# Two fused transformer blocks on one core: five places moved where one stage hands over to the next

## The chip, the cores and the metric

The kernel runs on one core of one Trainium2 chip. The metric is the device time of one execution in microseconds (us), as the median of several runs. All data is 32-bit.

## The reference, cut to what matters

Two blocks follow each other on 512 tokens of width 2048. Each block normalises its input, multiplies it with one very wide matrix, runs several mixers on slices of the product, and projects back.

```
# first block
p = rms_norm(x) @ w_in;  slices: lru, mlstm (u, o, z, ig, fg), moba (q, k, v, z)
ig = ig_pre + bi;  lf = log_sigmoid(fg_pre + bf)          # mlstm's two gates, 4 heads
uc = silu(causal_conv(u));  q, k = block_diag(uc, ..);  v = block_diag(u, ..)
x = x + concat(y_lru, y_ml, y_mo) @ w_out;  x = x + memory_cross_attention(x);  x = rms_norm(x)
# second block
proj = rms_norm(x) @ w_in_2;  slices: pool, swa, gla, mem, and g_logits (4 x 2048 columns)
y_c = gla_mixer(..)
gates = sigmoid(g_logits + b_merge)
merged = gates[0] * (y_a @ w_br_pool) + gates[1] * (y_b @ w_br_swa)
       + gates[2] * (y_c @ w_br_gla) + gates[3] * (y_m @ w_br_mem)
x = x + rms_norm(merged @ w_out_2)
```

## The kernel before, in words

**Split products.** Every large product is made in three passes. A weight tile `raw` (128 x 1024 numbers) is rounded by ScalarE (ACT) to `w_hi`; the rest, `w_lo = raw - w_hi`, is made by GpSimd (POOL, `low_rows`) in most stages and by VectorE (DVE, `w_low`) in the gate stage. The activations are split likewise into `ht_hi` and `ht_lo` (or `yh` and `yl`). TensorE (PE) then adds hi*hi, hi*lo and lo*hi.

**The ring.** `raw`, `w_hi` and `w_lo` have four slots each (`RING`). The tiles are numbered through the whole program (`PHASES`, `H4`), tile j lies in slot j % 4. `hi_done` counts ACT's roundings, `lo_done` the rests, `half_done` the tiles that PE has finished. SyncE (SP) issues the loads of `raw`, each when the rest of the tile four before it is made. Each engine has its own queue in program order, written by hand; no scheduler changes it. `PHASES` also counts, for each stage, the results that go through the two banks `proj0` and `proj1` in turn; `bank_free` counts when ACT or DVE has emptied them.

**The stages around the change**, in order of time:

- *mlstm, first pair of heads.* PE makes unit 0 and unit 1 of the projection; behind tile 9 of unit 1, `gate_picks` writes the two gates' rows to banks S0 and S1. ACT adds their bias (`r_ig`, `r_f`), takes the absolute value, the exponential and the logarithm (`r_b`, event `ln`), and only then the tanh of the convolved tile (`ml_th(0)`, line 1807) whose chunk DVE turns into `m_uc` (event `uc0`, line 2858). PE waits for `ln` and for `uc0` before `ml_qkv(0)` (line 928), which writes S0, S1 and S2.
- *zg, the branch product of the gla mixer.* Sixteen units of 8 tiles of contraction. The first three are begun on 6 tiles each (`early`: `proj0`, `proj1`, `t1`), since the last head's output is not there yet. `gla_out(3)`, eight transposes of `g_o`, stands behind the first of them. Behind the transposes DVE and ACT make the last two tiles of `yh` and `yl`. Unit 15 lies in `proj0`, the same bank into which the next stage, swa, puts its first unit; ACT empties each unit to `z_early` (line 2261) and spills it.
- *zp, the branch product of the pool mixer,* sixteen units, emptied to `z_late` (the fourth of each to `dist`, line 2261).
- *The gate stage.* g_logits is made in 32 pairs of column blocks. A pair takes seven products of half size (p1, p5, p6, p3, p7, p2, p4, line 1536) in place of eight, on sums of weight blocks (`t_w`) that DVE makes. ACT rounds the blocks and sums (`right_high`, `left_high`, lines 2493, 2497, 2527), DVE makes their rests (line 3559). Pairs use two sets of banks in turn. ACT rounds the three first tiles of pair 0 after it has emptied unit 15 of zp.
- *The closing product* merged @ w_out_2 (line 1582), 32 tiles in four blocks `fb` of 8 tiles `kp`. Its left operand `ht_hi`, `ht_lo` is `merged`, rounded by ACT (`merged_highs`, line 2567) and DVE (`lows`, line 3050). SP issues its first four loads after all of `gate_loads`, thus after the last `z_tile`. ACT rounds the first four tiles in the last pair (`merged_half`, line 2562), POOL makes their rests, and from tile 4 on ACT goes on after `phase_end`, at which ACT and DVE wait for each other.

The events of pair t that matter here: `lb11`, `lb22`, `lt3`, `lb21` say that slots 0, 1, 2 and 3 of `raw` have been read for the last time (for an odd b, slots 1 and 2 in this order).

Of the kernel before, what the change touches and what calls it, by code (L numbers as in the profile page):

```python
# [12 lines left out]
P = 128  # L13
T = 512
# [34 lines left out]
          ("xq", 8, 4), ("xwo", 8, 16), ("gv", 16, 2), ("gla", 32, 16), ("zg", 16, 16), ("swa", 80, 40),  # L49
# [80 lines left out]
def build(nc, a, out, stop=None):  # L130

    with ExitStack() as ctx:
# [376 lines left out]
        def _(sp):  # L509
# [151 lines left out]

            def gate_loads(m, b, first, last):
# [3 lines left out]
                if not last:  # L666
                    wait(sp, st_dve, "lb11", t)
                    gate_block(nm, nb, 0, 0, 0, block_in[0])
                    wait(sp, st_dve, "lb22", t + 1)
                    gate_block(nm, nb, slots[0], 0, 1, block_in[slots[0]])  # L670
                    wait(sp, st_dve, "lt3", t + 1)
                    gate_block(nm, nb, slots[1], 1024, 1, block_in[slots[1]])
# [6 lines left out]
                if not last:  # L679
                    wait(sp, st_dve, "lb21", t + 1)  # L680
                    gate_block(nm, nb, 3, 1024, 0, block_in[3])
# [11 lines left out]
            for fb in range(4):  # L693
                for kp in range(8):
                    j = 8 * fb + kp
                    if j < RING:
                        wait(sp, st_dve, ("lb11", "lb22", "lt3", "lb21")[j], PAIRS - 1 if j == 0 else PAIRS)
                    sp.wait_ge(lo_done, th(H4["wout2"], j) - RING)
                    sp.dma_start(raw[:, j % RING, :].rearrange("p (k n) -> p k n", n=T),
                                 a["w_out_2"][0][256 * kp:256 * kp + 256, T * fb:T * fb + T].rearrange(  # L700
                                     "(k p) n -> p k n", p=P)).then_inc(raw_ready[j % RING], 16)
# [7 lines left out]
        def _(pool):  # L709
# [34 lines left out]
            with pool.Fori(1, NH // RING) as i:  # L744
                low_rows(i)
# [3 lines left out]
        def _(pe):  # L749
# [155 lines left out]
            for pr in range(ML_PAIRS):  # L905
# [98 lines left out]
                if pr == 0:  # L1004
                    wait(pe, mlg_act, "ln")
# [355 lines left out]
            for u, bank in enumerate(early):  # L1361
# [4 lines left out]
                if u == 0:  # L1366
                    gla_out(GLA_HEADS - 1)
# [4 lines left out]
            with pe.Fori(1, 4) as i:  # L1372
                for u in range(4):
                    branch_unit(i + b, u, i * 2 + qb, u - 1, yh, yl)

# [230 lines left out]
        def _(act):  # L1606
# [174 lines left out]
            for pr in range(ML_PAIRS):  # L1781
# [90 lines left out]
                ml_th(0)  # L1872

                ml_ahead(2)
                ml_qv(0)
                ml_u(1)

                ml_th(1)
# [1828 lines left out]
```

## Time and profile before

| | |
|---|---|
| median of 3 runs | 3238.24 us (3236.93 to 3241.14) |
| the profiled execution's own time | 3237.58 us |
| its span, first to last instruction | 3235.8 us |
| PE busy | 3207.2 us, 99% |
| DVE, ACT, POOL busy | 1263.3, 1262.4, 1077.5 us |
| TensorE's granted clock, mean | 0.998 |
| share of PE in the chain that ended last | 96% |

PE is the engine that all others feed. "Busy" of PE is the time in which at least one matmul is in flight, so what the change could alter is PE's idle time, 28.6 us in all, and the rate of its matmuls. The list of waits names each of PE's pauses with the instruction that ended it; the chain that ended last gives start and length of each piece of work; the windows view gives the granted clock of a stretch, where 1.00 is 2.4 GHz and 0.50 is 1.2 GHz.

### The profile page before, as it was taken

The page shows a single profiled execution, that of the slowest core. Times are in us where ns is not written, and L with a number is a line of the kernel's source. Part 1 is how long each engine was busy: PE and PEld are TensorE (multiplying, and loading weights), DVE is VectorE, ACT ScalarE, POOL GpSimd, SP SyncE. Part 2 cuts the span into 40 slices and gives each one's busy share as a digit, 9 for nine tenths or more (in the row PEclk, how much of TensorE's full clock was granted, in tenths as well). Part 3 has the DMA queues.
Part 4 walks back from the last instruction along what each step waited for, and adds up shares of the span by engine and source line. Part 5 has one row for each costly group of instructions (what it writes and reads, how often), then busy time and mean ns, then how long its engine had stood idle before and what let it go on. Part 6 is the DMA issues. An engine that isn't in the chain of part 4 may idle for free.

```text
span 3235.8 us, 45156 instructions
## 1 busy us (share of the span) xinstructions
PE 3207.2 (99%) x17218; PEld 2757.1 (85%) x17218; DVE 1263.3 (39%) x1717; ACT 1262.4 (39%) x1928; POOL 1077.5 (33%) x464
## 2 busy tenths in 40 slices
PE   9999999999999999999999999999999999999999
PEld 8877888888888888888888888888889999999887
DVE  3573321112124544302110111135448888878701
ACT  6543322333236544332332333322334444444432
POOL 6633333434442434344343343444520000000143
PEclk9999999999999999999999999999999999999999
DMA  7622322323442423243332232423544444444442
GB/s 284 181 78 66 85 70 81 86 83 99 122 121 82 138 77 89 84 140 88 85 98 84 83 98 79 150 84 91 172 127 131 131 130 130 130 130 133 135 155 98
DMA packets 546541, 364.52 MB, mean 113 GB/s; under 512 B 18808, under 2 KB 505208, under 8 KB 545144
## 3 DMA queue, kind: packets, MB, share of 16 engines
q1 hardware_dynamic: 522912, 321.50, 34.1%
q10 hardware_dynamic: 23512, 41.40, 3.7%
q8 instruction: 81, 1.33, 0.2%
q14 instruction: 36, 0.29, 0.0%
HBM read 333.49 MB, written 29.36 MB: 112 GB/s over the span
## 4 chain that ended last, share of the span: by engine, by line
PE 96%; DVE 1%; ACT 1%; DMA 1%; issue 1%; POOL 0%; DVEq 0%; ACTq 0%; SPq 0%; POOLq 0%
PE proj L765 59%; PE s L1536 10%; PE t L1536 8%; PE s L1582 3%; PE s L1237 1%; PE proj L1582 1%; PE t L1582 1%; PE proj L1536 1%; PE t L790 1%; PE s L834 1%; PE s L827 1%; PE t L1237 1%; PE proj L1237 1%; PE s L1062 1%; PE s L1043 1%
## 5 line engine op out<-in xcount | busy, mean ns | idle before, releaser
L739 POOL TENSOR_TENSOR w_lo<-raw,w_hi 128x1024 fp32r<-128x1024 f32 x435 | 1075.4, 2486 | 2132.4 <-ACT w_hi L1619 1440.3
L765 PE MATMUL proj<-ht_hi,w_hi 128*128 128x512 f32 x2400 | 955.5, 398 | 0.7 <-ACT z_early L2261 0.7
L765 PE MATMUL proj<-ht_hi,w_lo 128*128 128x512 f32 x2400 | 935.5, 390 | 0.0
L765 PE MATMUL proj<-ht_lo,w_hi 128*128 128x512 f32 x2400 | 934.5, 389 | 0.0
L1619 ACT ACTIVATE w_hi<-raw 128x1024 fp32r<-128x1024 f32 x396 | 404.3, 1053 | 386.8 <-PE proj L765 223.3
L765 PEld LDWEIGHTS proj<-ht_hi,w_hi 128*128 128x128 f32 x2400 | 450.8, 188 | 95.8 <-issue 4.8
L765 PEld LDWEIGHTS proj<-ht_hi,w_lo 128*128 128x128 f32 x2400 | 450.4, 188 | 95.7
L765 PEld LDWEIGHTS proj<-ht_lo,w_hi 128*128 128x128 f32 x2400 | 451.0, 188 | 94.9 <-issue 4.6
L3559 DVE TENSOR_TENSOR w_lo<-raw,w_hi 128x1024 fp32r<-128x1024 f32 x128 | 156.4, 1222 | 73.0 <-ACT w_hi L2527 43.3
L1536 PE MATMUL s<-ht_hi,w_hi 128*128 128x256 f32 x512 | 145.4, 284 | 3.6 <-DVE w_lo L3559 3.6
L1536 PE MATMUL s<-ht_hi,w_lo 128*128 128x256 f32 x512 | 145.5, 284 | 0.0
L2497 ACT ACTIVATE w_hi<-t_w 128x1024 fp32r<-128x1024 f32 x96 | 101.4, 1057 | 112.7 <-DVE t_w L3575 58.4
L1536 PE MATMUL s<-ht_lo,w_hi 128*128 128x256 f32 x512 | 145.3, 284 | 0.0
L3559 DVE TENSOR_TENSOR w_lo<-t_w,w_hi 128x1024 fp32r<-128x1024 f32 x96 | 117.5, 1224 | 69.5 <-ACT w_hi L2497 69.5
L2493 ACT ACTIVATE w_hi<-raw 128x1024 fp32r<-128x1024 f32 x96 | 101.6, 1058 | 77.0 <-PE s L1536 38.9
L1536 PE MATMUL t<-ht_hi,w_lo 128*128 128x256 f32 x384 | 108.6, 283 | 0.0
L1536 PE MATMUL t<-ht_hi,w_hi 128*128 128x256 f32 x384 | 108.6, 283 | 0.0
L1536 PE MATMUL t<-ht_lo,w_hi 128*128 128x256 f32 x384 | 108.5, 282 | 0.0
L1536 PE MATMUL s<-s_hi,w_hi 128*128 128x256 f32 x384 | 108.1, 281 | 0.0
L1536 PE MATMUL s<-s_lo,w_hi 128*128 128x256 f32 x384 | 108.0, 281 | 0.0
L1536 PE MATMUL t<-s_hi,w_hi 128*128 128x256 f32 x384 | 108.0, 281 | 0.0
L1536 PE MATMUL t<-s_lo,w_hi 128*128 128x256 f32 x384 | 107.9, 281 | 0.0
(654 smaller groups left out, 5431.8 us busy)
## 6 DMA issues: line engine op xcount, KB each, us to landing
raw<-in_w_in_dram SPq DMA_DIRECT2D x404, 512.0 KB, 3.6
raw<-in_w_out_dram SPq DMA_DIRECT2D x64, 512.0 KB, 3.9
g_zt<-z_spill SPq DMA_DIRECT2D x64, 256.0 KB, 2.8
raw<-in_xa_wkv_dram SPq DMA_DIRECT2D x16, 512.0 KB, 7.7
raw<-in_w_mem_kv_dram SPq DMA_DIRECT2D x16, 512.0 KB, 3.8
raw<-in_w_br_gla_dram SPq DMA_DIRECT2D x16, 512.0 KB, 4.0
z_spill<-z_early ACTq DMA_DIRECT2D x32, 256.0 KB, 3.1
raw<-in_w_br_pool_dram SPq DMA_DIRECT2D x16, 512.0 KB, 4.2
```

What stands on the lines that cost most here:

```text
L739: pool.tensor_tensor(w_lo[:, slot, :], raw[:, slot, :], w_hi[:, slot, :].bitcast(F32), ALU.subtract).then_inc(lo_done, 1)
L765: ins = pe.matmul(dst, w, x[:, kt, c0:c1], start=first and n == 0 and m == 0, stop=last and n == len(kts) - 1 and m == 2)
L790: ins = pe.transpose(dst[0:m, n * P:n * P + k], src, ident[0:k, 0:k])
L827: pe.matmul(MEM_V[x][blk][:], h[:, kt, c0 + blk * P:c0 + blk * P + P], w, start=kt == 0 and m == 0, stop=kt == KT - 1 and m == 2)
L834: ins = pe.matmul(MEM_K[x][hd // 2][:, hd % 2 * M:hd % 2 * M + M], w, h[:, kt, c0:c0 + M], start=kt == 0 and hd % 2 == 0 and m == 0, stop= ...
L1237: ins = pe.matmul(VB[blk][t][:], x[:, kt, t * P:(t + 1) * P], w, start=kt == 0 and m == 0, stop=kt == KT - 1 and m == 2)
L1536: ins = pe.matmul(dst, w, x[:, k, :], start=fresh and k == 0 and m == 0, stop=k == 7 and m == 2, skip_group_check=True)
L1582: ins = pe.matmul(BANKS[fb % 2][t][:], x[:, k, t * P:(t + 1) * P], w, start=k == 0 and m == 0, stop=k == KT - 1 and m == 2)
L1619: act.activation(w_hi[:, slot, :], raw[:, slot, :], ACT.Copy).then_inc(hi_done, 1)
L2493: return act.activation(w_hi[:, (PRODUCTS * b + j) % RING, :], src, ACT.Copy)
L2497: return act.activation(w_hi[:, (PRODUCTS * b + j) % RING, :], t_w[:], ACT.Copy)
L3559: return dve.tensor_tensor(w_lo[:, slot, :], src, w_hi[:, slot, :].bitcast(F32), SUB)
```

## The change

1. **First gate pair.** ACT rounds the three first tiles of pair 0 behind units 12, 13 and 14 of zp, one each, in place of behind unit 15.
2. **Closing loads.** In the last pair, SP issues the first four loads of `w_out_2` one by one, each at the event that frees its slot, among the `z_tile` loads. The rests of these four tiles are made by DVE, not by POOL, which waits until they are made.
3. **Tanh ahead.** ACT makes `ml_th(0)` and rounds two tiles before the exponential and the logarithm; PE no longer waits for `ln`.
4. **Transposes.** `gla_out(3)` stands behind the second early unit.
5. **Bank.** Unit 15 of zg goes to `t1`; the two-bank stages count two units fewer, and the loop of zg is one turn shorter, its last turn written out.

```diff
-("zg", 16, 16)
+("zg", 16, 14)
@@ SP @@
-                if not last:
-                    wait(sp, st_dve, "lb11", t)
-                    gate_block(nm, nb, 0, 0, 0, block_in[0])
...
+                def load(slot, k0, n):
+                    if last:
+                        out_rows(slot)
+                    else:
+                        gate_block(nm, nb, slot, k0, n, block_in[slot])
+                wait(sp, st_dve, "lb11", t)
+                load(0, 0, 0)
+                wait(sp, st_dve, "lb22", t + 1)
+                load(slots[0], 0, 1)
+                wait(sp, st_dve, "lt3", t + 1)
+                load(slots[1], 1024, 1)
...
                 z_tile(m, b, 1)
+                wait(sp, st_dve, "lb21", t + 1)
+                load(3, 1024, 0)
...
-            for fb in range(4):
-                for kp in range(8):
...
+            for j in range(RING, 32):
+                sp.wait_ge(lo_done, th(H4["wout2"], j) - RING)
+                out_rows(j)
@@ POOL @@
-            with pool.Fori(1, NH // RING) as i:
+            with pool.Fori(1, H4["wout2"]) as i:
+                low_rows(i)
+            pool.wait_ge(lo_done, th(H4["wout2"], 3))
+            with pool.Fori(H4["wout2"] + 1, NH // RING) as i:
                 low_rows(i)
@@ PE @@
-                if pr == 0:
-                    wait(pe, mlg_act, "ln")
                 ml_qkv(0)
...
-                if u == 0:
+                if u == 1:
                     gla_out(GLA_HEADS - 1)
...
-            with pe.Fori(1, 4) as i:
+            with pe.Fori(1, 3) as i:
                 for u in range(4):
                     branch_unit(i + b, u, i * 2 + qb, u - 1, yh, yl)
+            for u in range(3):
+                branch_unit(b + 3, u, qb + 6, u - 1, yh, yl)
+            pe.wait_ge(z_apart, 1)
+            accumulate(b + 3, 3, TB[1][:], range(8), 0, yh, yl, (0, T), True, True)
@@ ACT @@
                     link(act.activation(r_b[0:4, :], r_f[0:4, :], ACT.Abs))
+                ml_th(0)
+
+                ml_ahead(2)
+                if pr == 0:
                     link(act.activation(r_b[0:4, :], r_b[0:4, :], ACT.Exp, scale=-1.0))
                     act.activation(r_b[0:4, :], r_b[0:4, :], ACT.Ln, bias=ones[0:4, 0:1]).then_inc(mlg_act.sem, 1)
-                ml_th(0)
-
-                ml_ahead(2)
...
+                    elif shift and isinstance(i, int) and i == 3 and u == 3:
+                        z_kept(st, TB[1], z_apart, 2, u, i * 4 + branch * KT + u, i + used)
...
-            act.sem_inc(bank_free[1], 1)
...
                     branch_z("zp", BR_POOL, i, (u,), 12, z_late)
+                    if 4 * i + u == 12:
+                        right_high(0, 0, B11, EARLIER + 16, block_in[0]).then_inc(st_act.sem, 9)
+                    elif 4 * i + u in (13, 14):
+                        wait(act, st_dve, ("t1", "t2")[u - 1], 0)
+                        left_high(0, u).then_inc(st_act.sem, u)
...
-            for slot in range(3):
-                act.wait_ge(half_done, th(H4["zp"], 12 + slot))
...
@@ DVE @@
-            lows(xy, HT_MERGED, 0.5, range(4))
+            def out_low(j):
+                dve.wait_ge(hi_done, th(H4["wout2"], j))
+                dve.tensor_tensor(w_lo[:, j, :], raw[:, j, :], w_hi[:, j, :].bitcast(F32), SUB).then_inc(lo_done, 1)
+            out_low(0)
+            out_low(1)
+            lows(xy, HT_MERGED, 0.5, range(2))
+            out_low(2)
+            lows(xy, HT_MERGED, 0.5, range(2, 4))
             corner(3, PAIRS, 4)
+            out_low(3)
             gated(1, GROUPS - 1, 3, PAIRS, 4, 1)
```

**ACT's queue at the end of zp and the start of the gate stage, before.** `z_late` and `dist` rows empty units 13, 14 and 15, each `DMA` spills one; L2493 and L2497 are `right_high` and `left_high`. The brackets name the semaphores that a row waits for (`x_in0` is the landing of the first weight block, `st_dve` is DVE's count of the gate stage).

```order
L2261 ACTIVATE z_late<-proj 128x512 [waits mem0_in1,half_done]
L2263 DMA z_spill<-z_late 128x512 [waits bank_free1]
L2261 ACTIVATE z_late<-proj 128x512 [waits mem0_in2,half_done]
L2263 DMA z_spill<-z_late 128x512 [waits bank_free0]
L2261 ACTIVATE dist<-proj 128x512 [waits mem0_in3,half_done]
L2263 DMA z_spill<-dist 128x512 [waits bank_free1]
L2493 ACTIVATE w_hi<-raw 128x1024 [waits x_in0,half_done]
L2497 ACTIVATE w_hi<-t_w 128x1024 [waits st_dve,half_done] x2
L2493 ACTIVATE w_hi<-raw 128x1024 [waits x_in2,half_done]
```

The same place of the changed program (line numbers of its own):

```order
L2276 DMA z_spill<-z_late 128x512 [waits bank_free0]
L2501 ACTIVATE w_hi<-raw 128x1024 [waits x_in0]
L2274 ACTIVATE z_late<-proj 128x512 [waits mem0_in1,half_done]
L2276 DMA z_spill<-z_late 128x512 [waits bank_free1]
L2505 ACTIVATE w_hi<-t_w 128x1024 [waits st_dve]
L2274 ACTIVATE z_late<-proj 128x512 [waits mem0_in2,half_done]
L2276 DMA z_spill<-z_late 128x512 [waits bank_free0]
L2505 ACTIVATE w_hi<-t_w 128x1024 [waits st_dve]
L2274 ACTIVATE dist<-proj 128x512 [waits mem0_in3,half_done]
L2276 DMA z_spill<-dist 128x512 [waits bank_free1]
L2501 ACTIVATE w_hi<-raw 128x1024 [waits x_in2,half_done]
```

The first three roundings have moved ahead of the emptying of units 13, 14 and 15; the fourth stays behind it.

**ACT's queue at the gates of mlstm, before.** `ACT_TABLE_LOAD` is the switch between function tables that the compiler puts in.

```order
L1869 ACTIVATE r_b<-r_f 4x512 [waits act_chain]
L1870 ACT_TABLE_LOAD
L1870 ACTIVATE r_b<-r_b 4x512 [waits act_chain]
L1871 ACT_TABLE_LOAD
L1871 ACTIVATE r_b<-r_b,ones 4x512 [waits act_chain]
L1807 ACT_TABLE_LOAD
L1807 ACTIVATE m_h<-m_uc 128x512 [waits ml_conv]
L1619 ACTIVATE w_hi<-raw 128x1024 [waits half_done,raw_ready2]
L1619 ACTIVATE w_hi<-raw 128x1024 [waits half_done,raw_ready3]
L1815 ACTIVATE m_q<-s 128x512 [waits ml_pe]
L1803 ACTIVATE m_up<-proj 128x512 [waits ml_dve,ml_pe,half_done]
L1807 ACTIVATE m_h<-m_uc 128x512 [waits ml_conv]
```

And of the changed program:

```order
L1881 ACTIVATE r_b<-r_f 4x512 [waits act_chain]
L1819 ACT_TABLE_LOAD [waits ml_conv]
L1819 ACTIVATE m_h<-m_uc 128x512 [waits act_chain]
L1631 ACTIVATE w_hi<-raw 128x1024 [waits half_done,raw_ready2]
L1631 ACTIVATE w_hi<-raw 128x1024 [waits half_done,raw_ready3]
L1886 ACTIVATE r_b<-r_b 4x512
L1887 ACT_TABLE_LOAD
L1887 ACTIVATE r_b<-r_b,ones 4x512 [waits act_chain]
L1827 ACTIVATE m_q<-s 128x512 [waits ml_pe]
L1815 ACTIVATE m_up<-proj 128x512 [waits ml_dve,ml_pe,half_done]
L1819 ACT_TABLE_LOAD
L1819 ACTIVATE m_h<-m_uc 128x512 [waits ml_conv]
```

Three table switches stay three, but only one now stands ahead of the first tanh, and it carries the wait for the convolution (`ml_conv`) itself. The exponential has none of its own any more.

**DVE's queue at the end of the last gate pair, before.** L3624 and L3626 are the last two sums of the pair, L3050 the rests of `merged`, L3583 the corner sum that needs p4.

```order
L3624 TENSOR_TENSOR t<-t,dist 128x256 [waits st_act,st_pe]
L3626 TENSOR_TENSOR t<-t,dist 128x256 [waits st_pe]
L3050 SCALAR_TENSOR_TENSOR ht_lo<-xy,ht_hi 128x512 [waits norm_hi] x4
L3583 TENSOR_TENSOR t<-proj,sn_188 128x256 [waits st_pe]
L3593 SCALAR_TENSOR_TENSOR g_zt_187<-gate_e,g_zt_187 128x512 [waits z_in1,st_act]
L3595 TENSOR_TENSOR xy<-xy,g_zt_187 128x512 [waits st_dve]
```

And of the changed program:

```order
L3635 TENSOR_TENSOR t<-t,dist 128x256 [waits st_act,st_pe]
L3637 TENSOR_TENSOR t<-t,dist 128x256 [waits st_pe]
L3653 TENSOR_TENSOR w_lo<-raw,w_hi 128x1024 [waits hi_done] x2
L3061 SCALAR_TENSOR_TENSOR ht_lo<-xy,ht_hi 128x512 [waits norm_hi] x2
L3653 TENSOR_TENSOR w_lo<-raw,w_hi 128x1024 [waits hi_done]
L3061 SCALAR_TENSOR_TENSOR ht_lo<-xy,ht_hi 128x512 [waits norm_hi] x2
L3594 TENSOR_TENSOR t<-proj,sn_188 128x256 [waits st_pe]
L3653 TENSOR_TENSOR w_lo<-raw,w_hi 128x1024 [waits hi_done]
L3604 SCALAR_TENSOR_TENSOR g_zt_187<-gate_e,g_zt_187 128x512 [waits z_in1,st_act]
```

Four rests of weight tiles, POOL's before, stand in DVE's queue among the rests of `merged` and around the corner sum.

## Rows read from the trace of the kernel before

**Rows 1.** The page: POOL's rests and the commonest matmul; busy us, mean ns of one, idle before.
```profile
L739 POOL TENSOR_TENSOR w_lo<-raw,w_hi 128x1024 fp32r<-128x1024 f32 x435 | 1075.4, 2486 | 2132.4 <-ACT w_hi L1619 1440.3
L765 PE MATMUL proj<-ht_hi,w_hi 128*128 128x512 f32 x2400 | 955.5, 398 | 0.7 <-ACT z_early L2261 0.7
```
**Rows 2.** The list of PE's waits: line, what ended it, us in total, times, longest.
```profile
PE s L1582 <- DVE ht_lo L3050: 4.8, 1, 4.8
PE s L928 <- DVE m_uc L2858: 4.1, 1, 4.1
PE s L1536 <- DVE w_lo L3559: 3.6, 1, 3.6
...
PE s L790 <- DVE g_o L3244: 1.7, 1, 1.7
...
PE proj L765 <- ACT z_early L2261: 0.7, 1, 0.7
```
**Rows 3.** Windows of 2 us: PE, PEld, DVE, ACT, POOL busy, granted clock, DMA share, GB/s.
```profile
248.00:250.00 2.00, 2.00 (x4) 0.91 (x3) 0.00 (x0) 0.00 (x0) 2.00 (x2) 0.50 0.00 0
1372.00:1374.00 2.00, 1.23 (x10) 1.19 (x11) 0.81 (x3) 0.00 (x0) 0.00 (x0) 1.00 0.00 0
2408.00:2410.00 2.00, 2.00 (x11) 2.00 (x11) 0.80 (x2) 1.22 (x2) 0.00 (x0) 0.50 0.67 200
3054.00:3056.00 2.00, 2.00 (x6) 1.53 (x5) 2.00 (x1) 1.85 (x3) 1.72 (x2) 0.50 0.33 126
```
**Rows 4.** The chain that ended last (start, us): first and second gate pair's opening part.
```profile
2406.35 21.72 PE s L1536 x168
...
2448.07 20.00 PE s L1536 x168
```
**Rows 5.** Timeline of DVE and ACT at the end of zp (start, us).
```profile
2377.63 2.85 DVE L3565 TENSOR_TENSOR t_w<-raw 128x1024 f32<-128x1024 f32 x1 [15.42 <-DMA raw<-in_w_in_dram]
...
2403.89 1.06 ACT L2493 ACTIVATE w_hi<-raw 128x1024 fp32r<-128x1024 f32 x1 [0.49 <-ACT dist L2261]
```
**Rows 6.** The chain that ended last, closing product: its first load, blocks fb 0 and 2.
```profile
3041.60 6.49 DMA raw<-in_w_out_dram
...
3052.86 45.38 PE s L1582 x192
...
3141.75 43.52 PE s L1582 x192
```
**Rows 7.** Timeline of DVE and ACT in and behind the last gate pair.
```profile
3029.80 1.22 DVE L3559 TENSOR_TENSOR w_lo<-raw,w_hi 128x1024 fp32r<-128x1024 f32 x1
...
3049.70 2.18 ACT L2567 ACTIVATE ht_hi<-xy 128x512 fp32r<-128x512 f32 x4
...
3063.39 4.90 DVE L3050 SCALAR_TENSOR_TENSOR ht_lo<-xy,ht_hi 128x512 fp32r<-128x512 f32 x8
```
**Rows 8.** Timeline of ACT and DVE at the gates of mlstm, and a switch in lru.
```profile
210.67 1.28 ACT L1746 ACT_TABLE_LOAD   x1 [2.37 <-PE proj L765]
...
239.46 2.33 DVE L2751 SCALAR_TENSOR_TENSOR m_uc<-m_up,par,m_uc 128x512 f32<-128x512 f32 x3
...
243.75 1.28 ACT L1807 ACT_TABLE_LOAD   x1
245.04 0.63 ACT L1807 ACTIVATE m_h<-m_uc 128x512 f32<-128x512 f32 x1
245.71 0.69 DVE L2858 SCALAR_TENSOR_TENSOR m_uc<-m_h,m_uc 128x512 f32<-128x512 f32 x1 [3.92 <-ACT m_h L1807]
```
**Rows 9.** The chain that ended last: `ml_qkv(0)` of the first and of the second pair.
```profile
246.54 4.51 PE s L928 x6
...
374.93 2.58 PE s L928 x6
```
**Rows 10.** Timeline of DVE behind the transposes of `gla_out(3)`.
```profile
1373.90 1.41 DVE L3253 SCALAR_TENSOR_TENSOR y_f<-s,par,g_z 128x512 f32<-128x512 f32 x2 [1.19 <-PE s L790]
1375.36 1.35 DVE L3258 TENSOR_TENSOR yl<-y_f,yh 128x512 fp32r<-128x512 f32 x2
```

More of the change, by code:

```diff
@@ L48 @@
 PHASES = [("kv", 32, 2), ("lru", 16, 8), ("ml", 36, 18), ("moba", 48, 24), ("wout", 32, 16),
-          ("xq", 8, 4), ("xwo", 8, 16), ("gv", 16, 2), ("gla", 32, 16), ("zg", 16, 16), ("swa", 80, 40),
+          ("xq", 8, 4), ("xwo", 8, 16), ("gv", 16, 2), ("gla", 32, 16), ("zg", 16, 14), ("swa", 80, 40),
           ("mem", 16, 8), ("zs", 8, 16), ("pool", 32, 16), ("zm", 8, 16), ("zp", 16, 16), ("wout2", 32, 16)]
@@ L660, in _, with out_rows @@
                 gate_block(0, 0, slot, k0, n, block_in[slot])
+            def out_rows(j):
+                fb, kp = j // 8, j % 8
+                sp.dma_start(raw[:, j % RING, :].rearrange("p (k n) -> p k n", n=T),
+                             a["w_out_2"][0][256 * kp:256 * kp + 256, T * fb:T * fb + T].rearrange(
+                                 "(k p) n -> p k n", p=P)).then_inc(raw_ready[j % RING], 16)
             def gate_loads(m, b, first, last):
@@ L665, in gate_loads @@
                 slots = (2, 1) if b % 2 == 0 else (1, 2)
-                if not last:
-                    wait(sp, st_dve, "lb11", t)
-                    gate_block(nm, nb, 0, 0, 0, block_in[0])
[L669 to L672, printed above, removed]
+                def load(slot, k0, n):
[9 more added lines that the diff above has]
+                load(slots[1], 1024, 1)
                 if first:
@@ L678, in gate_loads @@
                 z_tile(m, b, 1)
-                if not last:
-                    wait(sp, st_dve, "lb21", t + 1)
-                    gate_block(nm, nb, 3, 1024, 0, block_in[3])
+                wait(sp, st_dve, "lb21", t + 1)
+                load(3, 1024, 0)
                 if not first:
@@ L692, in _ @@
                 gate_loads(GROUPS - 1, b, False, b == 3)
-            for fb in range(4):
-                for kp in range(8):
[L695 to L701, printed above, removed]
+            for j in range(RING, 32):
+                sp.wait_ge(lo_done, th(H4["wout2"], j) - RING)
+                out_rows(j)
             for n, (t, c0, c1) in enumerate(OUT_PARTS):
@@ L2482, in sums_high @@
                 act.activation(sums[n][0], sums[n][1], ACT.Copy).then_inc(sums_hi, 1)
-            for i in range(4):
-                for u in range(4):
-                    branch_z("zp", BR_POOL, i, (u,), 12, z_late)
-                    if 3 <= 4 * i + u < 7:
-                        sums_high(4 * i + u - 3)
             def right_high(b, j, src, value, landed):
@@ L2502, in gate_tanh @@
                                       bias=par[:, bass.ds(m * 2 + x + PARAM["b_merge"] + b * KT, 1)])
-            for slot in range(3):
-                act.wait_ge(half_done, th(H4["zp"], 12 + slot))
-                if slot == 0:
-                    right_high(0, 0, B11, EARLIER + 16, block_in[0]).then_inc(st_act.sem, 9)
-                else:
-                    wait(act, st_dve, ("t1", "t2")[slot - 1], 0)
-                    left_high(0, slot).then_inc(st_act.sem, slot)
+            for i in range(4):
+                for u in range(4):
+                    branch_z("zp", BR_POOL, i, (u,), 12, z_late)
+                    if 3 <= 4 * i + u < 7:
+                        sums_high(4 * i + u - 3)
+                    if 4 * i + u == 12:
[3 more added lines that the diff above has]
+                        left_high(0, u).then_inc(st_act.sem, u)
             def gate_pair(m, b, first=False, last=False):
```

## The prediction

> **What bounds the kernel now.** PE has work in flight for 3207.2 of 3235.8 us, so nothing can be won on the other engines except where PE waits for them. I read four views in this order. First the page, for the shape of a matmul [rows 1]. Then the list of PE's waits: five pauses lie at the places that the change touches, 4.8, 4.1, 3.6, 1.7 and 0.7 us, 14.9 us together, half of PE's 28.6 us of idle time [rows 2]. Then the granted clock behind each pause, which the wait list does not show: it is 0.50 for some us behind the 4.1, 3.6 and 4.8 us pauses, so PE runs at 1.2 in place of 2.4 GHz there, but 1.00 behind the 1.7 us pause [rows 3]. Last the chain and the timelines at each place, for what a pause costs in the work behind it and for what would be late next.
>
> A second thing that the wait list hides: a matmul is 0.398 us long in the records [rows 1], but 192 of them take 43.52 us, 0.227 each [rows 6]. A pause is counted from the end of the last one, so closing it also takes back the overlap, 0.398 - 0.227 = 0.17 us. I use it for each pause that closes whole.
>
> **Part 1, first gate pair.** Today ACT empties unit 15, rounds the first tile at 2403.89 for 1.06 us, DVE makes the rest, and PE stands still for 3.6 us [rows 2, 5]. In the changed queue this rounding stands behind unit 12. A unit is 24 matmuls, some 5.5 us, so it starts three units earlier, near 2387. What it needs is there: DVE had both first weight blocks at 2377.63 and made their difference by 2380.5 [rows 5]. The two sums follow at units 13 and 14, again with 5.5 us for about 1.1 us of ACT and 2.4 of DVE, which has nothing else to do. So the pause goes, 3.6 + 0.17. Behind it the seven products of pair 0 took 21.72 us, those of pair 2 took 20.00 [rows 4]: 1.72 us of half clock, which goes too, since PE no longer stops. Together **5.5 us**. SP's loads of the next blocks move ahead with `lb11`, so nothing behind gets later.
>
> **Part 2, closing loads.** Now the first load of `w_out_2` is issued after the last `z_tile`, at 3041.6, and ACT cannot go on until the second has landed near 3048.1 [rows 6]. It then makes `ht_hi` at 3049.70 [rows 7], DVE the rest, PE waits 4.8 us [rows 2]. With the change the slot of tile 0 is free before the last pair begins (3028), and the slot of tile 1 at about 3031.0, when DVE has made the `lb22` rest that starts at 3029.80 [rows 7]; even at 6.5 us a load both are in by 3037.5. ACT may round tile 0 after p3 and tile 1 after p7, which ends two products of 20.00 / 7 us [rows 4] before p4, near 3042.4; DVE then makes its last sum of the pair. p4 ends at 3048.1 (3052.86 less 4.8) [rows 2, 6]. From there: tile 1 rounded by 3043.5, tanh 0.7, four `ht_hi` of 0.54 each [rows 7] by 3046.4. DVE is free from 3042.8: two rests of 1.22 us [rows 7] to 3045.2, then the first two `ht_lo` at some 0.6 us each, done by 3046.5. So there is 1.5 us to spare and the pause closes, 4.8 + 0.17. The first block of the closing product took 45.38 us against 43.52 of a later one [rows 6]: 1.86 us of half clock, gone as well. Together **6.8 us**. What is late next: the second `kp` needs `ht_lo` 2 and 3, which now stand behind the rest of tile 2. This tile can be rounded after p2 and the first four `ht_hi`, by 3047.4, so `ht_lo` 3 is done near 3049.8, and PE wants it 24 matmuls after 3048.1, at 3053.5. POOL's four rests leave a queue that did nothing else.
>
> **Part 3, tanh ahead.** The pause ends at 246.54 and was 4.1 us, so it began at 242.45 [rows 2, 9]. ACT went through two more table switches, exponential and logarithm before it could switch to tanh at 243.75 (1.28 us) and compute it (0.63 us); DVE's `m_uc` took 0.69 us, PE started 0.14 us later [rows 8]. The convolution that tanh needs was ready at 239.46 + 2.33 = 241.79 [rows 8]. In the new queue the one switch left carries the wait for it. A switch behind such a wait does not run ahead: in lru it began when PE was done [rows 8]. So 241.8 + 1.28 + 0.63 + 0.69 and 0.2 of hand-overs gives 244.6: the pause shrinks from 4.1 to 2.2 us, **1.9 us** won. Behind it `ml_qkv(0)` took 4.51 us at half clock against 2.58 at full [rows 3, 9], 1.93 us. Whether that is won depends on a pause of 2.2 us, which this trace does not have: 1.7 us did not lower the clock, 3.6 us did [rows 2, 3]. Between 0 and **1.9 us** I take 1.9, since 2.2 is nearer to 1.7. The exponential and logarithm end near 248.5 and are wanted only after the second convolution; if the clock stays up, ACT's copy of q comes 1.2 us after PE's products, beside unit 2's 10.9 us.
>
> On the price of a switch the Trainium skill differs (ScalarE: Activation LUTs, What ACT_TABLE_LOAD costs): it adds 1.38 us of drain to each switch, 2.66 us in all. By that figure the pause would stay at 3.5 us. The rows have no room for it: the load of 1.28 us at 243.75 is followed by tanh at 245.04 [rows 8]. The measurement decides.
>
> **Parts 4 and 5.** DVE's `g_o` came 1.7 us after PE's first early unit [rows 2]; now 18 matmuls of 0.227, 4.1 us, lie between, so the pause goes, 1.9 us with the overlap. Late next could be the last two `yl`: they were ready 2.8 us after the transposes (1373.90 to 1376.71) [rows 10], and one early unit of 4.1 us is left to cover them. It covers, with 1.3 us over. Unit 15 in `t1` frees `proj0` two units early, which ends the 0.7 us pause, 0.9 with the overlap. Together **2.8 us**. ACT, DVE and SP have the same rows as before there.
>
> **The sum.** 5.5 + 6.8 + 1.9 + 1.9 + 2.8 = 18.9 us off the profiled execution, 3237.6 to 3218.7. That execution lies 0.7 us under the median, so the forecast for the median is 3238.2 - 18.9 = **3219.3 us**.
>
> **The rivals.**
> *The clock falls behind the shortened mlstm pause.* For it: three of the four pauses I priced are followed by half clock, and 2.2 us is over the longest that was not. Against: it is much nearer to 1.7 than to 3.6. It costs 1.9 us: 3221.2. *A switch behind a wait costs a second length of itself,* some drain of the engine. Then the pause stays at 3.5 us and the clock falls as it did: 1.3 + 1.9 us over the forecast, 3222.5. The rows speak against it: the tanh starts 0.01 us after its switch [rows 8]. The drain that the Trainium skill gives (ScalarE: Activation LUTs, What ACT_TABLE_LOAD costs) would be this case.
> *One joint keeps its pause,* because a wait takes the removed one's place: the likeliest is the closing one, where three engines must all be on time with 1.5 us to spare. If its pause and clock stay whole, 3219.3 + 6.8 = 3226.1; if it is the gate pair, 3224.8. Each us of a partial failure costs one us.
> *It gets slower.* The place is tile 4 of the closing product. ACT rounds it only after `phase_end`, thus after DVE's whole queue, to which four rests are added (4.9 us). PE wants it 96 matmuls after 3048.1, at 3069.9; DVE's queue used to end at 3068.3 [rows 7], which with ACT's rounding of 1.06 and POOL's rest of 2.49 us [rows 1, 5] would come too late. But it used to start its rests of `merged` at 3050.4 and now starts at 3042.8, so I have its end at 3062. From about 3065.5 on each us is lost. It would take an end near 3090 to make the kernel slower than 3244.7, which needs DVE or a load to hang for 28 us. I see nothing that would.
> *The switch still runs ahead of its wait,* against what the queue says: then the pause is 0.9 us and the time 3218.0.
>
> **How the numbers follow.** All joints close and the clock stays up: 0.50, 3219.3. The clock falls after the mlstm pause: 0.28, 3221.2. The longer switch: 0.03, 3222.5. One joint keeps all or part of its pause: 0.12, 3222 to 3226.1. Switch ahead: 0.03. Slower: 0.02. Two hundredths are left for something unseen that eats most of the gain. The three runs of before spread over 4 us, so a median may sit 1.5 us off on either side. The range from 3216.0 to 3225.5 holds all cases but the rare ones and the whole failure of the largest joint. The measurement can tell 0.2%, 6.5 us, from no change. Every case but the last two lies below 3231.8: faster 0.94, same 0.04, slower 0.02.
>
> **What would show it.** In the list of PE's waits the entries for L1582, L1536, `g_o` and `z_early` are gone, and the one for `ml_qkv` reads 2.2 us. The first gate pair's opening part takes 20.0 us, the first closing block 43.5, `ml_qkv(0)` 2.6. PE's idle time falls from 28.6 to about 15.9 us. I am wrong if a new wait over 0.5 us stands at the third early unit of zg, at the second or fifth `kp` of the closing product, or if the granted clock still reads 0.50 behind a joint.

## The result, and the profile after

The changed kernel takes **3217.24 us** (median of 4 runs, 3216.34 to 3218.66), the kernel before beside it 3238.41 us (4 runs, 3236.93 to 3241.14): a ratio of 0.9934, 95% interval 0.9917 to 0.9951. The forecast was 3219.3 us with a range from 3216.0 to 3225.5. The profiled execution of the changed kernel took 3218.66 us with a span of 3216.5, that of before 3237.58 and 3235.8. So the traces differ by 19.3 us where the sum said 18.9. One later run of the kernel before, in the third set of experiments, was slow (3985.86 us at a mean granted clock of 0.752) and is left out of every median and ratio here.

The list of PE's waits after the change, in the columns of [rows 2]:

```profile
PE s L859 <- POOL small L739: 3.0, 1, 3.0
PE s L938 <- DVE m_uc L2869: 2.1, 1, 2.1
PE s L800 <- DVE ht_lo L2674: 0.9, 1, 0.9
PE t L800 <- ACT a_pt L1955: 0.5, 1, 0.5
PE s L800 <- DVE ht_lo L2682: 0.5, 1, 0.5
```

Of the five pauses of [rows 2], four are gone; `ml_qkv`'s is left with 2.1 us in place of 4.1. The 3.0 us at the top stood in the kernel before too, and so did, with 1.5 us, the third line: the chain leads there from the landing of one of the first weight tiles (`raw<-in_xa_wkv_dram`, at 38.17 us here and 38.98 before) through ACT and DVE to PE, and no part of the change is near. Below, this wait is called the first landing.

The chain that ended last (start us, us, what) says where each microsecond was won:

```profile
243.76 2.84 PE s L938 x6
246.60 10.90 PE proj L775 x48
...
370.48 2.58 PE s L938 x6
...
2395.40 19.99 PE s L1548 x168
...
2435.39 20.00 PE s L1548 x168
...
3035.39 43.55 PE s L1594 x192
...
3122.46 43.52 PE s L1594 x192
```

Such rows are read by how far each landmark lies ahead of the same one in before. The `ml_qkv(0)` of the second pair is 4.45 us earlier (374.93 to 370.48 [rows 9]); 0.81 us of it was there before mlstm began, from the first landing, so mlstm gave 3.64. The first gate pair begins 10.95 us earlier (2406.35 to 2395.40 [rows 4]). 2.91 us of that came in zg, and the rest, 3.6, is the gate pair's pause. The second gate pair is 12.68 us earlier (2448.07 to 2435.39), so the opening part behind the joint gave 1.73 more. The closing product starts 17.47 us earlier (3052.86 to 3035.39 [rows 6]), 4.79 from its own pause, and its block 2 is 19.29 us earlier (3141.75 to 3122.46), another 1.82 from the first block. PE's record of busy time fell from 3207.2 to 3201.1 us although it does the same matmuls. Most of these 6.1 us is work that ran at half clock, the rest mainly the overlap at each joint; no list of waits shows either.

ACT at the gates of mlstm in the changed kernel (start us, us, and in brackets the idle time ahead and what ended it), to be put beside [rows 8]:

```profile
238.31 0.63 ACT L1881 ACTIVATE r_b<-r_f 4x512 f32<-4x512 f32 x1
241.06 1.28 ACT L1819 ACT_TABLE_LOAD   x1 [2.11 <-DVE m_uc L2762]
242.35 0.63 ACT L1819 ACTIVATE m_h<-m_uc 128x512 f32<-128x512 f32 x1
242.88 1.99 ACT L1631 ACTIVATE w_hi<-raw 128x1024 fp32r<-128x1024 f32 x2
244.78 0.61 ACT L1886 ACTIVATE r_b<-r_b 4x512 f32<-4x512 f32 x1
245.41 1.28 ACT L1887 ACT_TABLE_LOAD   x1
```

ACT is idle for 2.11 us and only then loads its table: the load stands behind the wait for the convolution, as in lru. The exponential at 244.78, behind the tanh, has no load of its own; before the change it had one. The logarithm, with its load at 245.41, lies beside PE's products.

DVE and ACT in the last gate pair, same columns, beside [rows 7]:

```profile
3030.01 2.35 DVE L3653 TENSOR_TENSOR w_lo<-raw,w_hi 128x1024 fp32r<-128x1024 f32 x2
3032.28 1.28 DVE L3061 SCALAR_TENSOR_TENSOR ht_lo<-xy,ht_hi 128x512 fp32r<-128x512 f32 x2
...
3043.60 4.90 DVE L3061 SCALAR_TENSOR_TENSOR ht_lo<-xy,ht_hi 128x512 fp32r<-128x512 f32 x8
```
```profile
3031.20 2.18 ACT L2578 ACTIVATE ht_hi<-xy 128x512 fp32r<-128x512 f32 x4
3033.28 1.05 ACT L2573 ACTIVATE w_hi<-raw 128x1024 fp32r<-128x1024 f32 x1
```

The first two `ht_lo` are done at 3033.56, and in the chain PE's closing product starts at 3035.39, 1.8 us later (its first matmul is at 3035.23, 1.7 us later; the section on the prediction says where the difference comes from). DVE's queue ends at 3048.50.

### The profile page after: what moved, and what is told of

The parts are those of the page before. It is cut to its first block, busy times and chain, and to the rows that moved or that the text cites. A ratio compares the mean times of both kernels' runs of the same rounds, so it can differ in the third digit from the quotient of the medians.

```text
span 3216.5 us, 45137 instructions
## 1 busy us (share of the span) xinstructions
PE 3201.1 (100%) x17218; PEld 2754.0 (86%) x17218; DVE 1261.3 (39%) x1721; ACT 1262.4 (39%) x1928; POOL 1068.2 (33%) x460
## 4 chain that ended last, share of the span: by engine, by line
PE 97%; DVE 1%; DMA 1%; ACT 1%; issue 0%; POOL 0%; SPq 0%; DVEq 0%; ACTq 0%; POOLq 0%
PE proj L775 59%; PE s L1548 10%; PE t L1548 9%; PE s L1594 3%; PE proj L1548 1%; PE proj L1594 1%; PE s L1245 1%; PE t L1594 1%; PE t L800 1%; PE s L844 1%; PE s L837 1%; PE t L1245 1%; PE proj L1245 1%; DMA raw<-in_xa_wkv_dram 1%; PE s L1070 1%; PE s L1051 1%
```

## The experiments

Each set ran on one chip with the kernel before beside it: 3237.21 us in the first set, 3237.87 in the second, 3236.93 in the third. Medians of 5 or 6 runs; "pause" is the wait at the joint concerned, in the profiled execution.

| kernel | median us (range) | ratio to before (95%) | pause us |
|---|---|---|---|
| again | 3219.55 (3216.94 to 3220.70) | 0.9947 (0.9934 to 0.9961) | mlstm 2.1 |
| u_gate | 3224.16 (3222.21 to 3225.53) | 0.9961 (0.9948 to 0.9975) | gate pair 3.6 |
| u_close | 3227.19 (3224.60 to 3227.57) | 0.9969 (0.9957 to 0.9981) | closing 4.7 |
| u_tanh | 3222.13 (3221.20 to 3224.71) | 0.9955 (0.9942 to 0.9969) | mlstm 4.1 |
| u_zg | 3222.19 (3221.37 to 3223.28) | 0.9953 (0.9939 to 0.9966) | zg 1.7 and 0.7 |
| c_pool | 3218.74 (3217.77 to 3220.08) | 0.9941 (0.9928 to 0.9955) | closing none |
| p_two | 3221.39 (3220.95 to 3223.15) | 0.9950 (0.9937 to 0.9964) | mlstm 3.4 |
| x_sel | 3217.66 (3216.11 to 3217.94) | 0.9937 (0.9924 to 0.9951) | mlstm 1.7 |
| again2 | 3219.97 (3218.98 to 3220.15) | 0.9945 (0.9931 to 0.9959) | mlstm 2.1 |
| x_exp | 3217.30 (3215.62 to 3217.89) | 0.9936 (0.9922 to 0.9950) | mlstm 0.9 |
| x_both | 3217.11 (3215.61 to 3218.50) | 0.9938 (0.9924 to 0.9953) | mlstm 0.7 |

None of them leaves out any part of the reference. The sets are: again, u_gate, u_close and u_tanh on one chip; u_zg, c_pool, p_two and x_sel on a second; again2, x_exp and x_both on a third. The second set has no run of the changed kernel.

### again: the changed kernel once more, for the size of the scatter

> The changed kernel once more, beside the runs that undo one part each. Theory: each joint gives its pause, 0.17 us of overlap and, for pauses of 3.6 us and more, 1.7 to 1.9 us of half clock; ratio to before 0.994 (19 to 21 us). Rival: the fast runs of before and after differ by chance and the pauses alone count; then 14 us, ratio 0.9957.

3219.55 us, 2.3 over its median of the first measurement; its single runs go from 3216.94 to 3220.70. The gain over the kernel before is 17.7 us, under the 19 to 21 that were expected, and the interval of the ratio holds both the theory's 0.994 and the rival's 0.9957. So the medians do not decide between them. A difference of 1 us between two medians says nothing here, and the parts below are read from the traces first.

### u_gate: part 1 undone

```diff
-                    if 4 * i + u == 12:
-                        right_high(0, 0, B11, EARLIER + 16, block_in[0]).then_inc(st_act.sem, 9)
...
+            for slot in range(3):
+                act.wait_ge(half_done, th(H4["zp"], 12 + slot))
```

> Part 1 undone: the first three tiles of gate pair 0 are rounded behind unit 15 of zp again. Theory: 5.5 us over the changed kernel, a pause of 3.6 us and the first pair's opening part at 21.7 us with a granted clock of 0.50 in it. Rival, pauses alone count: 3.8 us over, opening part at 20.0. Rival, a later wait takes it up: under 2 us.

4.6 us over the changed kernel of the same set, and the pause of 3.6 us is back whole. The half clock behind it is not. The chain of u_gate:

```profile
243.08 4.22 PE s L938 x6
247.30 11.24 PE proj L775 x48
...
2399.99 20.24 PE s L1548 x168
```

Its windows of 2 us (as in [rows 3]), at mlstm and behind the gate pause:

```profile
244.00:246.00 2.00, 2.00 (x4) 0.86 (x3) 0.00 (x0) 1.98 (x3) 2.00 (x2) 0.60 0.00 0
...
2400.00:2402.00 2.00, 2.00 (x17) 2.00 (x18) 1.90 (x2) 0.00 (x0) 0.00 (x0) 1.00 0.44 97
2402.00:2404.00 2.00, 2.00 (x19) 2.00 (x18) 0.79 (x2) 1.57 (x2) 0.00 (x0) 1.00 0.57 166
```

Behind the same pause of 3.6 us, which in the profile of before had the clock down [rows 3, 4], the clock reads 1.00 here. The opening part is 0.25 us longer than the changed kernel's 19.99, and that is no half clock either: 0.16 of it is the overlap that the chain cuts off a piece that follows without a pause (see the section on the prediction), and the first matmul behind the pause is 0.36 us long in place of 0.28. The 2.1 us pause in mlstm, behind which the clock held in the changed kernel, cost 1.7 here: 4.22 against 2.84 in `ml_qkv(0)` and 11.24 against 10.90 in the piece behind it. So this execution fits the rival "pauses alone count" (3.8 us, opening part near 20.0) and not the theory's 5.5; the rest of what the profile is over comes from mlstm and from the first landing. What stands behind a pause of one length differs from profile to profile.

### u_close: part 2 undone

```diff
+                if not last:
+                    wait(sp, st_dve, "lb11", t)
+                    gate_block(nm, nb, 0, 0, 0, block_in[0])
...
-            out_low(0)
-            out_low(1)
-            lows(xy, HT_MERGED, 0.5, range(2))
...
+            lows(xy, HT_MERGED, 0.5, range(4))
```

> Part 2 undone whole: the four closing loads are issued behind the last z_tile, and POOL makes their rests. Theory: 6.8 us over the changed kernel, a pause of 4.8 us, first closing block 45.4 us. Rival, pauses alone count: 5.0 us over, first block 43.5 us.

7.6 us over the changed kernel of the set. Its wait at the closing product, and its chain:

```profile
PE s L1588 <- DVE ht_lo L3055: 4.7, 1, 4.7
```
```profile
3028.64 5.59 DMA raw<-in_w_out_dram
3039.79 45.45 PE s L1588 x192
3128.76 43.52 PE s L1588 x192
```

Read as in the prediction, 4.7 + 0.17 + 1.93 is 6.8, the size that it gave the part. Read by landmarks it is 6.6: u_close is 0.29 us ahead of the changed kernel inside the last gate pair (3015.10 against 3015.39) and 6.30 behind it at block 2 (3128.76 against 3122.46). The section on the prediction says where the 0.2 us between the two readings come from. The 1 us to 7.6 is within what medians scatter.

### u_tanh: part 3 undone

```diff
+                if pr == 0:
+                    wait(pe, mlg_act, "ln")
...
-                ml_th(0)
-
-                ml_ahead(2)
```

> Part 3 undone: exponential and logarithm ahead of the first tanh, and PE waits for the logarithm. Theory: 3.8 us over the changed kernel, pause 4.1 us in place of 2.1, ml_qkv(0) 4.5 us in place of 2.8 at a granted clock of 0.50. Rival, the clock is indifferent: 2.0 us over, ml_qkv(0) unchanged.

2.6 us over the changed kernel. The trace shows the pause of 4.1 us again, `ml_qkv(0)` at 4.51 us, and a granted clock of 0.60 and 0.55 in the two windows behind it: 2.0 us of pause and 1.7 of half clock, 3.7 in all. The median shows less. It may be that some executions of the changed kernel pay the half clock too, as u_gate above and c_pool below do at this place; but its own three profiles do not show it, so this is not shown.

### u_zg: parts 4 and 5 undone

```diff
-                if u == 1:
+                if u == 0:
...
-            pe.wait_ge(z_apart, 1)
-            accumulate(b + 3, 3, TB[1][:], range(8), 0, yh, yl, (0, T), True, True)
```

> Parts 4 and 5 undone: the transposes behind the first early unit, unit 15 of zg in proj0. Theory: 2.8 us over the changed kernel, pauses of 1.7 and 0.7 us back, granted clock 1.00 throughout there. Rival, the eight transposes only change places and the wait for the last two tiles of yl takes the pause over: 1 us over.

3222.19 us, 3.5 over c_pool of the same set, which has the changed kernel's joints. The 1.7 us before `g_o` and the 0.7 us before `z_early` are back. Against the trace of the changed kernel the two cost 2.9 us, so the rival of 1 us fell.

### c_pool: the closing loads early, but POOL makes the four rests

```diff
-            with pool.Fori(1, H4["wout2"]) as i:
-                low_rows(i)
-            pool.wait_ge(lo_done, th(H4["wout2"], 3))
-            with pool.Fori(H4["wout2"] + 1, NH // RING) as i:
+            with pool.Fori(1, NH // RING) as i:
...
-            out_low(0)
-            out_low(1)
```

> Half of part 2: the closing loads stay early, but POOL makes the rests of the first four tiles as before. Theory: the loads were what was late. POOL needs 2.5 us a rest, tile 0 is there by 3025, tile 1 some 0.3 us before p4 ends, so PE starts on time or at most 0.5 us late: 0 to 0.5 us over the changed kernel. Rival: the gain needs DVE, since POOL's passes and DVE's rests of merged slow each other (1.46 us each in place of 0.6 in the trace of before): pause of 1 to 3 us.

3218.74 us, no closing pause, first block 43.55 us. POOL's first rest ended at 3032.11 and not by 3025, early enough all the same, and the rival's pause of 1 to 3 us did not come. Part 2's gain is that of the loads. Moving the four rests to DVE is not needed for it, though it leaves more room: the first two `ht_lo` were done 0.9 us ahead of PE's first closing matmul, in place of 1.7. Beside POOL's rests DVE's first four `ht_lo` took 5.93 us here (timeline of DVE, then of POOL, in c_pool):

```profile
3033.61 5.93 DVE L3058 SCALAR_TENSOR_TENSOR ht_lo<-xy,ht_hi 128x512 fp32r<-128x512 f32 x4 [1.75 <-ACT ht_hi L2575]
3042.98 2.49 DVE L3058 SCALAR_TENSOR_TENSOR ht_lo<-xy,ht_hi 128x512 fp32r<-128x512 f32 x4
```
```profile
3032.55 2.41 POOL L746 TENSOR_TENSOR w_lo<-raw,w_hi 128x1024 fp32r<-128x1024 f32 x1 [0.45 <-ACT w_hi L2570]
3036.16 2.83 POOL L746 TENSOR_TENSOR w_lo<-raw,w_hi 128x1024 fp32r<-128x1024 f32 x1 [1.20 <-ACT w_hi L2570]
```

The next four, with POOL idle, took 2.49 us. Of the first four only two are long, 1.90 and 2.90 us; each ends some 0.55 us after one of POOL's rests. The two between them, which started with POOL idle, took 0.68 each. c_pool's windows behind its mlstm pause of 2.1 us show the clock down again:

```profile
244.00:246.00 2.00, 2.00 (x3) 0.67 (x2) 0.00 (x0) 1.98 (x3) 2.00 (x1) 0.50 0.00 0
246.00:248.00 2.00, 2.00 (x5) 0.87 (x3) 0.00 (x0) 1.28 (x2) 2.00 (x2) 0.65 0.24 40
```

In the changed kernel the same windows read 1.00:

```profile
244.00:246.00 2.00, 2.00 (x5) 0.81 (x5) 0.00 (x0) 1.98 (x3) 2.00 (x1) 1.00 0.00 0
246.00:248.00 2.00, 2.00 (x9) 1.50 (x8) 1.29 (x2) 1.99 (x4) 2.00 (x2) 1.00 0.17 36
```

Up to this place the two programs do the same work in the same order. Nor is it the chip: u_zg ran on the chip of c_pool, and again and u_close on that of u_gate, and in these three the clock held. The six products of `ml_qkv(0)` took 4.54 us in c_pool and 2.84 in the changed kernel.

### p_two: the tanh of the first pair made three times

```diff
-                ml_th(0)
+                ml_th(0, 2 if pr == 0 else 0)
```

> A doubled cost: the tanh of ml_th(0) is made three times over in the first pair, which lengthens PE's pause there from 2.1 to 3.4 us and changes nothing else. Theory, the length of the pause decides the clock: at 3.4 us the granted clock falls to 0.50 behind it as it did at 3.6, and the kernel is 1.3 + 1.9 = 3.2 us over the changed one. Rival, the clock falls behind the heavy engine switch only at 3.6 us and more: 1.3 us over, ml_qkv(0) still 2.8 us.

The pause is 3.4 us, 1.3 longer, which is two tanh of 0.63, so ACT's work there is on the path one to one; `ml_qkv(0)` took 4.54 us and the clock read 0.92, 0.50 and 0.73 in the three windows from 244 to 250. The median, 3221.39, is 2.65 us over that of c_pool. The run does not say that the length of the pause decides: behind 2.1 us, in c_pool, the clock fell as well and `ml_qkv(0)` took the same 4.54 us.

### x_sel: two small preparations of DVE behind the first convolution

```diff
-            link.inc(dve.tensor_copy(i_r[:], ident[:]))
-            link.inc(dve.tensor_tensor(r_sel[:], ident[:, 0:4], ident[:, 32:36], ADD))
...
+                if pr == 0:
+                    link.inc(dve.tensor_copy(i_r[:], ident[:]))
+                    link(dve.tensor_tensor(r_sel[:], ident[:, 0:4], ident[:, 32:36], ADD))
```

> A further step: DVE's two small tiles (i_r, r_sel, 2.5 us, of which r_sel 2.35 beside POOL) go behind the first convolution. Theory: PE's pause before ml_qkv(0) is bound by the convolution's end at 241.0; it starts 2.4 us earlier, then ACT's absolute value at 238.9 and the switch are last, and the pause falls from 2.1 to under 0.2 us: 2.0 us under the changed kernel. Rival: POOL's passes slow the convolution too where it now runs beside them (2.33 us for three passes becomes 4 or more), and the pause stays at 1 us or over.

A miss: the pause went from 2.1 only to 1.7 us. `r_sel` is an addition of 128x4 numbers that takes 2.35 us where it stands, so to take it off the path should have been worth 2. But once it is moved, the next instruction is as long. DVE in x_sel:

```profile
234.05 2.68 DVE L2760 TENSOR_SCALAR m_uc<-m_up,par 128x512 f32<-128x512 f32 x1
236.77 2.33 DVE L2762 SCALAR_TENSOR_TENSOR m_uc<-m_up,par,m_uc 128x512 f32<-128x512 f32 x3
...
241.87 0.16 DVE L2942 TENSOR_TENSOR r_sel<-ident 128x4 fp32r<-128x4 f32 x1
```

POOL in x_sel, same columns:

```profile
231.70 4.75 POOL L746 TENSOR_TENSOR w_lo<-raw,w_hi 128x1024 fp32r<-128x1024 f32 x2 [15.08 <-ACT w_hi L1631]
```

The pass that takes 0.55 us elsewhere takes 2.68 here and ends at 236.73, just behind the end of POOL's rests at 236.45; `r_sel`, at its new place with POOL idle, takes 0.16. So the time was POOL's and not `r_sel`'s: the next instruction of the convolution took its place beside POOL's rest and was stretched instead. That is the rival, POOL slowing the convolution, though the pass that it slowed is the first and not the three that were expected (2.33 us as before). All clock times of this profile lie 1.5 us ahead of the changed kernel's from the first landing on (POOL's two rests begin at 231.70 against 233.19), so the convolution, which ends at 239.10 against 240.98, gained 0.4 us by the move.

### again2, x_exp and x_both: the exponential ahead of the tanh

The first is the changed kernel. In x_exp the exponential of the gate moves ahead of the tanh, so that its table is there before the wait; x_both has x_sel's move as well.

```diff
+                    link(act.activation(r_b[0:4, :], r_b[0:4, :], ACT.Exp, scale=-1.0))
                 ml_th(0)

                 ml_ahead(2)
                 if pr == 0:
-                    link(act.activation(r_b[0:4, :], r_b[0:4, :], ACT.Exp, scale=-1.0))
```

> The changed kernel once more, beside the next two. If the clock behind the 2.1 us mlstm pause is a matter of the execution, as the profiles so far read (ml_qkv(0) 2.84, 2.84, 2.84 and 4.22, 4.54 us), its runs spread over some 3 us between 3216.5 and 3220.5, with a median of 3217.2 to 3219.6.

> The exponential of the gate stands ahead of the tanh, the logarithm stays behind it. In the trace of the changed kernel the exponential that follows the tanh has no table switch between, so the two share a table. Theory (the switch behind the wait is what is left of the pause, 1.28 of 2.1 us): the switch now runs ahead of the wait, tanh starts when the convolution ends, the pause is 0.8 to 0.9 us, the clock does not fall, ml_qkv(0) takes 2.6 to 2.9 us, and the median is 1.3 to 2.5 us under the changed kernel's of this set. Rival (tanh and exponential need different tables in this order, or the switch follows the wait whatever stands ahead): the pause stays at 2.1 us or grows to 2.7, and the median is level with the changed kernel's or over it.

> The same, and i_r and r_sel behind the first convolution as well, which let it end 1.9 us earlier. Theory: ACT is then the last to be ready, abs, switch, exponential and tanh from 238.3 on (0.63 + 1.28 + 0.63 + 0.63), so m_uc is ready near 242.3 and the pause is 0.3 to 0.8 us; the median is 0 to 0.5 us under that of the kernel with the exponential alone, and 1.5 to 3 us under the changed kernel's. Rival (DVE, slowed down beside POOL, is what ends the pause): the pause is that of the kernel with the exponential alone or longer, and the median no better than its.

ACT in x_exp:

```profile
239.25 1.28 ACT L1882 ACT_TABLE_LOAD   x1
240.55 0.63 ACT L1882 ACTIVATE r_b<-r_b 4x512 f32<-4x512 f32 x1
241.39 0.63 ACT L1819 ACTIVATE m_h<-m_uc 128x512 f32<-128x512 f32 x1 [0.21 <-DVE m_uc L2762]
```

PE's waits in x_exp:

```profile
PE s L800 <- DVE ht_lo L2674: 1.1, 1, 1.1
PE s L938 <- DVE m_uc L2869: 0.9, 1, 0.9
```

The table is loaded while DVE still convolves, tanh starts as soon as the convolution ends, and the pause falls from 2.1 to 0.9 us: the 1.28 us of the load were what was left of it above tanh and `m_uc`. The clock read 1.00 behind it and the six products took 2.84 us. All five runs of x_exp (3215.62 to 3217.89) lie below all five of the changed kernel beside it (3218.98 to 3220.15). The medians are 2.7 us apart, a little more than expected, but the changed kernel has also run at 3216.34, and the two intervals overlap; what is shown is the 1.2 us of pause. x_both's pause is 0.7 us and its median no different from x_exp's. ACT is then the last to be ready, as expected, though by 0.3 us only: the 1.9 us by which x_sel's convolution was expected to end earlier were 0.4 and the first landing. again2 itself missed what was expected of it: a spread of some 3 us and a median of at most 3219.6, against a spread of 1.2 and a median of 3219.97. x_exp is the version to keep: it does x_both's work with one move less.

## Why the prediction was right, step by step

**The overlap of 0.17 us per closed pause** is there, but the prediction counted it twice at the gate pair and at the closing product. The chain lets a joined piece begin where the record ahead of it ends, at 2395.40; the timeline of PE has the gate pair's first matmul already at 2395.24:

```profile
2395.01 0.39 PE L775 MATMUL proj<-yp_hi,w_lo 128*128 128x512 f32 x1
2395.24 0.28 PE L1548 MATMUL s<-ht_hi,w_hi 128*128 128x256 f32 x1
```

By this start the closed pause gave 3.75 us and not 3.6, and the half clock 1.57 and not 1.73; the closing joint likewise (first matmul at 3035.23) 4.95 and 1.66. The pieces that the prediction took for its full-clock prices, 20.00, 43.52 and 2.58 us, are such joined pieces, each shorter by the overlap than if it were read from its first matmul, as a piece behind a pause is. So its differences 1.72, 1.86 and 1.93 each hold 0.17 that is no half clock; for the first two it had added the same 0.17 to the pause, and at mlstm, where a pause stays, nothing is won by it. Zg's two pauses of 1.7 and 0.7 us gave 2.9 with the overlap, which is counted once there.

**Part 1, 5.5 us, measured 5.3**. ACT rounded the three tiles behind units 12, 13 and 14, at 2379.71, 2385.26 and 2390.91, each followed by DVE's rest. The first is the prediction's 2387 less the 7.4 us won before it. Nothing became late. The 0.2 us are the overlap counted twice. The half clock in it is that of one pair of executions, though, and this is where the prediction had luck: u_gate had the pause and no half clock behind it.

**Part 2, 6.8 us, measured 6.6**, again with the overlap counted twice. The rival "one joint keeps its pause" fell. Where 1.5 us to spare were predicted, 1.8 were measured, and DVE's queue ended at 3048.5, which is 12.7 us (what had been won before the last joint) below 3061.2 on the clock of before, where the prediction had 3062. That settles the slower rival too. c_pool adds that the loads alone carry the gain.

**Part 3, 1.9 + 1.9 us, measured 2.0 + 1.7.** The switch carried the wait: at 241.06, 0.08 us after the convolution's end at 240.98, with 1.28 us and tanh right behind at 242.35. With switch, tanh and `m_uc` behind the convolution the predicted pause was 2.2 us, and 2.1 were read. The rival of the longer switch fell; tanh again starts 0.01 us behind its load, and the 1.38 us of drain that the Trainium skill adds (ScalarE: Activation LUTs, What ACT_TABLE_LOAD costs) has no place in these rows. The half-clock term was 0.2 too large: at a granted clock of 1.00 `ml_qkv(0)` of the first pair is 2.84 us long in the chain (in all six profiles with a pause of 2.1 or 1.7 us before it), not the 2.58 of the second. PE's timeline of the changed kernel, behind the pause and in the second pair, settles where the 0.26 us come from:

```profile
243.76 0.70 PE L938 MATMUL s<-m_uc,m_bd 128*128 128x512 f32 x1 [2.11 <-DVE m_uc L2869]
...
370.31 0.59 PE L938 MATMUL s<-m_uc,m_bd 128*128 128x512 f32 x1
```

The second pair's products begin at 370.31 and not at the chain's 370.48, which is the overlap of 0.17 once more, and the first matmul behind a pause is 0.1 us longer.

**The first rival, the clock behind the shortened pause,** came true in some profiles and not in others. With a pause of 2.1 us the clock held in five profiles (the changed kernel three times, u_close, u_zg) and fell in two (c_pool, u_gate). What a fall costs is best read from the start of `ml_qkv(0)` to the start of the second one: 14.18 us in the changed kernel, 15.89 in u_gate and 15.88 in c_pool, and as much behind the longer pauses: 15.85 in before, 15.88 in u_tanh, 15.90 in p_two. So a fall costs 1.7 us each time. The prediction gave this rival 0.28 as a property of the kernel. The five programs of these seven profiles do the same work up to this pause, and on each of two chips one profile held and another fell, so it looks like a matter of the execution; no single program was profiled both with and without the fall, so that stays an inference. That the changed kernel's first profile had none of it was luck in part.

The first landing explains more of the scatter: PE's wait for the first `ht_lo` was 0, 0.9 and 2.1 us in the three profiled executions of the changed kernel, which took 3216.94, 3218.66 and 3220.02 us and show no other difference of that size.

**Parts 4 and 5, 2.8 us, measured 2.9.** `g_o` was ready at 1368.34 and the transposes began at 1370.62; the last `yl` was ready at 1374.50, and PE went on to the last two tiles at 1375.59 without a wait, 1.1 us to spare where 1.3 were predicted.

**The sum** was 18.9, the traces give 19.3. In the 19.3 are 0.81 us of the first landing, which the change does not touch, so the change itself gave 18.5; the 0.4 us less are in the main the overlap in the half-clock terms, and that this and the landing lie close together is luck. The gains in the medians, 21.2 us in the first measurement, 17.7 in again and 17.0 in again2, lie on both sides of it.

**What stays open:** why the clock falls behind one pause of 2.1 us and not behind the next. No kernel here was made to settle it; with the pause at 0.9 us (x_exp) and 0.7 (x_both) the one profile of each shows no fall.

## What to carry to other kernels

When PE is nearly always busy, list its waits, and price each as its length plus the overlap of two matmuls plus the half-clock work that may, and in some executions does not, stand behind it (here behind pauses of 2.1 us and longer, 1.6 to 1.7 us each time). Measure the half-clock work between two starts of matmuls, not between pieces of the chain, or the overlap is counted twice. A joint closes when what it needs can be made some units earlier from data that are already there; then check what is next in line on each engine. On ACT look at which function stands ahead of a wait: one that shares the table of the function behind it takes the table load off the path.

## What the runs showed of the hardware that was not expected

- Some DVE instructions beside a POOL rest of 128x1024 end only when that rest ends or up to 0.55 us later, whatever their size: 128x4 in 2.35 us against 0.16 alone, a 128x512 pass in 2.68 against 0.55, two `ht_lo` in 1.90 and 2.90 against 0.68. A tiny instruction that shows as long is a sign of its neighbour, and to move it can move the delay on to the next.
- Not every DVE instruction is held so. In the changed kernel `m_k`, read from bank `s`, took 0.69 us in the midst of POOL's rests (0.67 with POOL idle), and a MEMSET of 128x256 beside them took 0.27:

```profile
246.64 0.69 DVE L2873 TENSOR_SCALAR m_k<-s 128x512 f32<-128x512 f32 x1 [2.94 <-PE s L938]
```
```profile
244.00 4.72 POOL L746 TENSOR_TENSOR w_lo<-raw,w_hi 128x1024 fp32r<-128x1024 f32 x2 [5.99 <-ACT w_hi L1631]
```

  The held rows above take all their inputs from working tiles and none from a bank; no run was made to tell which property decides.
- The granted clock behind a pause of the same length is not the same in each profile: behind 3.6 us it fell in before and held in u_gate, behind 2.1 us it fell twice and held five times. Where it fell it cost 1.6 to 1.7 us, behind 2.1 us as behind 4.8.
- Tanh and exponential followed one another without a table load in either order (the exponential at 244.78 in the changed kernel, as its queue already showed, and the tanh at 241.39 in x_exp); in both the logarithm behind them needed one.
